# Silu of the normalised rows kept in its PSUM bank instead of an SBUF tile

## The reference

```
hn = rms_norm(x, norm_g)
a, b, gate = split(hn @ w_in, 3)                  # w_in 1024 x 3072
u = a * sigmoid(b)
u = depthwise causal conv (31 taps) of u + conv_b
u = (u - mean) * rsqrt(var + 1e-5) * ln_g + ln_b   # over the channels
u = silu(u) * silu(gate)
y = x + u @ w_out                                  # w_out 1024 x 1024
```

## The kernel before

| bank held by | passes to |
|---|---|
| `norm` 0, h = 0 | unit 23, half 0 |
| `norm` 1, 2, 3, h = 0 | `norm` 4, 5, 6, h = 0 |
| `norm` 4, h = 0 | unit 23, half 1 |
| `norm` 5, 6, h = 0 | `norm` 0, 1, h = 1 |
| `norm` 7, h = 0 | output `q` = 4 |
| `norm` k, h = 1 | `norm` k + 2, h = 1 |

## Time and profile before

### The profile page before, as it was taken

One profiled execution on the slowest core, in us unless ns is written; L12 is line 12 of the kernel. 1 busy time (PEld: TensorE's weight loads), 2 busy tenths in 40 slices (PEclk: granted clock), 3 DMA queues, 4 the chain that ended last, 5 costly groups with the idle time before them and its releaser, 6 DMA issues.

```text
span 387.0 us, 4783 instructions
## 1 busy us (share of the span) xinstructions
PE 377.4 (98%) x1704; PEld 305.5 (79%) x1704; DVE 277.4 (72%) x432; ACT 197.0 (51%) x301; POOL 243.2 (63%) x179
## 2 busy tenths in 40 slices
PE   3999999999999999999999999999999999999997
PEld 2788888888888888888888888888887888888886
DVE  4848899999998988999999999476248574011011
ACT  6869765576467517764685666444574650000000
POOL 0325999999999985999999999943423620000000
DMA  7993013111011111011111011110303558110111
GB/s 276 399 403 137 3 56 108 54 57 38 16 56 55 55 56 54 5 52 54 57 55 44 13 53 54 57 54 0 110 0 108 181 199 301 56 54 36 48 54 54
DMA packets 12263, 34.07 MB, mean 88 GB/s; under 512 B 1360, under 2 KB 1872, under 8 KB 12240
## 3 DMA queue, kind: packets, MB, share of 16 engines
q1 hardware_dynamic: 11952, 33.56, 24.2%
q10 hardware_dynamic: 288, 0.21, 0.3%
HBM read 29.57 MB, written 4.19 MB: 87 GB/s over the span
## 4 chain that ended last, share of the span: by engine, by line
PE 96%; DVE 1%; DMA 1%; ACT 0%; issue 0%; ACTq 0%; DVEq 0%
PE mm L433 64%; PE acc L506 17%; PE mm L506 7%; PE mm L450 5%; PE mm L489 2%; PE mm L500 2%; DMA ident<-identity 1%; DVE x_lo L818 1%; PE acc L427 1%; DVE w_lo L826 0%; ACT x_hi L570 0%; DVE nat L1031 0%; ACTq L558 0%; DVEq L817 0%
## 5 line engine op out<-in xcount | busy, mean ns | idle before, releaser
L433 PE MATMUL mm<-x_lo,w_hi 128*128 128x512 f32 x352 | 139.6, 397 | 0.0
L433 PE MATMUL mm<-x_hi,w_hi 128*128 128x512 f32 x352 | 139.3, 396 | 0.0
L433 PE MATMUL mm<-x_hi,w_lo 128*128 128x512 f32 x352 | 139.2, 396 | 0.0
L902 DVE SCALAR_TENSOR_TENSOR acc<-u,chan,acc 128x512 f32<-128x512 f32 x154 | 108.4, 749 | 0.1
L433 PEld LDWEIGHTS mm<-x_hi,w_hi 128*128 128x128 f32 x352 | 66.1, 188 | 16.1
L433 PEld LDWEIGHTS mm<-x_lo,w_hi 128*128 128x128 f32 x352 | 66.1, 188 | 15.6
L433 PEld LDWEIGHTS mm<-x_hi,w_lo 128*128 128x128 f32 x352 | 66.1, 188 | 15.5
L1102 POOL TENSOR_TENSOR pconv<-pconv,prod 128x512 f32<-128x512 f32 x60 | 77.3, 1313 | 0.4 <-ACT prod L658 0.4
L902 DVE SCALAR_TENSOR_TENSOR acc<-u,w_sum,acc 128x512 f32<-128x512 f32 x90 | 67.4, 749 | 0.2
L1065 POOL TENSOR_TENSOR w_lo<-raw,w_hi 128x1024 fp32r<-128x1024 f32 x21 | 51.0, 2427 | 20.5 <-ACT w_hi L608 20.4
L1102 POOL TENSOR_TENSOR pool_before<-pool_before,prod 128x512 f32<-128x512 f32 x41 | 53.5, 1304 | 1.6
(11 more groups left out here) (86 smaller groups left out, 449.9 us busy)
## 6 DMA issues: line engine op xcount, KB each, us to landing
raw<-w_in SPq DMA_DIRECT2D x22, 512.0 KB, 3.3
nat<-x_t SPq DMA_DIRECT2D x16, 256.0 KB, 6.1
sgate<-x SPq DMA_DIRECT2D x8, 512.0 KB, 10.7
raw<-w_out SPq DMA_DIRECT2D x8, 512.0 KB, 3.3
nat<-x SPq DMA_DIRECT2D x8, 512.0 KB, 6.0
y<-nat SPq DMA_DIRECT2D x15, 256.0 KB, 2.0
raw<-w_in SPq DMA_DIRECT2D x4, 256.0 KB, 4.7
y<-nat SPq DMA_DIRECT2D x2, 128.0 KB, 1.8
```

Of the source, the lines that this page charges most:

```text
L433: ins = nc.tensor.matmul(bank(("unit", m, h)), w[:, m % 3, k, :], xx[:, k, half(h)], start=(k == 0 and i == 0), stop=(k == KC - 1 and i == 2))
L902: ins = nc.vector.scalar_tensor_tensor(dst, chain_in(j, chain, k), tap(j, chain, k), chain_bank(j, chain), ALU.mult, ALU.add)
```

## The change

Silu is written over its own input, in the PSUM bank. The gate's product reads it from there. The wait for a free slot of `sig` is gone. The bank of a `norm` job is now released by the gate's product on DVE (`v_ready`, same count) and no longer by the Silu on ACT (`actv_ready`). No instruction is added, removed or moved on any engine; only operands and waits differ. The `sig` tile stays, since the first product's sigmoid uses it.

```diff
@@ release(job)
-            return actv_ready, KC * h + n + 1
+            return v_ready, KC * h + n + 1
@@ act_norm(k, h), ScalarE
                 act.wait_ge(nt_ready, n + 1)
-                if n >= 2:
-                    act.wait_ge(v_ready, n - 1)
-                nc.scalar.activation(sig[:, n % 2, :], bank(("norm", k, h)), ACT.Silu, scale=ln_g[:, k:k + 1],
+                nc.scalar.activation(bank(("norm", k, h)), bank(("norm", k, h)), ACT.Silu, scale=ln_g[:, k:k + 1],
                                      bias=ln_b[:, k:k + 1]).then_inc(actv_ready, 1)
@@ gate(k, h), VectorE
                 dve.wait_ge(actv_ready, n + 1)
                 dve.wait_ge(g_read, NH * k + h + 1)
-                nc.vector.tensor_tensor(sgate[:, k, part], sig[:, n % 2, :], sgate[:, k, part],
+                nc.vector.tensor_tensor(sgate[:, k, part], bank(("norm", k, h)), sgate[:, k, part],
                                         ALU.mult).then_inc(v_ready, 1)
```

## The result

The changed kernel took 390.14 us (median of 10 runs, 389.8 to 391.1), the kernel before 389.33 us (median of 10, 388.69 to 390.0). The ratio is 1.0022, its 95% interval 1.0012 to 1.0033: a little slower, +0.8 us, with an interval of +0.5 to +1.3 us. I had forecast +0.6 us and a time of 389.9 us in a range of 389.2 to 390.8. The difference is clear of zero, but the interval holds the bound of 0.2% (0.78 us) that the forecast had set between no change (0.49) and slower (0.45), so it does not settle on which side of it the change lies.

A forecast was written before the change was run, and what follows sets the result against it. PE, busy 98% of the span, was taken to bound the kernel. Two new waits less the absorbed gap, +0.58 + 0.57 - 0.54 = +0.61 us, gave 389.42 us profiled, 389.9 us median, range 389.2 to 390.8.

The forecast's parts named there:

- The sign, the place and the mechanism: Slower by 0.61 us, because PE newly waits for DVE's gates at both halves of unit 23.
- The absorbed gap: Before the output stage, PE's 0.54 us loss to late `x_lo` of k = 0 is given back.
- The rival that paid both waits in full: Gap before the output stage is really issue and stays: +1.15 us, 390.45 us; chance 0.22.
- S1: PE's new wait at unit 23 half 0 for the gate of k = 0: 0.58 us.
- S2: PE's new wait at unit 23 half 1 for the gate of k = 4: 0.57 us, on top of S1.
- the sum of +0.61: Whole kernel: two new waits at unit 23 less the gap before the output stage, +0.58 + 0.57 - 0.54 us.
- how far `x_lo` moves: Before the output stage, `x_lo` of k = 0 ends 0.27 us later, at 290.84 us.
- two passes: Rival: in-place Silu reads and writes its PSUM bank in turn, 1.27 us; +2.9 us, 392.2 us; chance 0.08.
- Not slower: Rival: unit 23's banks are free in time, only the earlier ACT remains; 388.5 us profiled, 389.0 median; chance 0.08.
- The other banks: Remaining `norm` banks at both h: released early enough, no further PE wait; nearest in h = 1 has some 1.7 us slack.
- the faster gates: Gates of h = 1 beside POOL fall from up to 2.49 to 0.69 us, hidden behind busy PE, worth nothing.

The follow-up runs named there:

- Experiment 1: Kernel before with only the bank release moved to the gate's product, Silu still to SBUF; median 390.10 us, ratio 1.0015.
- experiment 2: Changed kernel, but Silus of k = 0 and 4, h = 0, go to `sig` and release their banks themselves; median 389.22 us, ratio 0.9998.
- experiment 3: Changed kernel, but only the Silu of k = 4, h = 0, goes to `sig` and releases its bank; median 389.74 us, ratio 1.0013.
- experiment 4: Changed kernel, but only the Silu of k = 0, h = 0, goes to `sig` and releases its bank; median 389.63 us, ratio 1.0001.
- experiment 5: Kernel before with ScalarE's third and fourth `w_out` splits placed behind two and four `x_hi`; median 388.87 us, ratio 0.9993.
- experiment 6: Changed kernel with ScalarE's third and fourth `w_out` splits placed behind two and four `x_hi`; median 389.98 us, ratio 1.0021.
- Experiment 8: Changed kernel, but at unit 23 PE waits first for the bank, then for the weights' low part; 390.6 us in one run.

## Why the prediction was right, point by point

**The sign, the place and the mechanism held.** PE waits for the gates of k = 0 and k = 4, at the two places named, and for no other gate. Experiment 1 shows that the release alone makes the difference, experiment 2 that without the two waits it is gone.

**The absorbed gap held.** I had read the 0.31 us of "issue" as `x_lo` of k = 0 behind POOL, a loss of 0.54 us that one of the two waits would fill. Measured: -0.55 us, and experiments 3, 4 and 5 each show it from another side. The rival that paid both waits in full is out in the kernel as it is: that would be M = 15.48 + 1.28 = 16.76. Both waits in full, 1.28 us, are what experiments 5 and 6 differ by, once the gap has been removed.

**Mis-sized: S1 and S2.** They were 0.58 and 0.57 us, and are 0.64 each. The step that was too small is the time from DVE's end to the weight load. I took 0.06 us from the earlier trace rows; at unit 23 it is 0.12 (279.04 to 279.16). Experiment 8 shows that this depends on the order in which the two semaphores are waited for: the earlier trace rows is a wait behind one semaphore, unit 23 one behind two with the late one second. Why the order matters no run shows. The Silu's 0.04 us of shortening was 0.024 (776 to 752 ns), and the gates started 0.02 to 0.03 us earlier. Per wait that is some 0.07 us more than forecast, of which 0.06 to 0.07 show (0.64 against 0.58 and 0.57). With the gap's 0.55 in place of 0.54 it makes the 0.12 us by which M (+0.73) missed the sum of +0.61.

**Mis-sized, without effect: how far `x_lo` moves.** I had +0.27 us; from the first transpose to the end of `x_lo` of k = 0 it is 15.08 us before and 15.46 after, +0.38. Of the 0.11 us between them 0.06 are those of S1, 0.02 those of the Silus (0.29 us earlier and not 0.31), and 0.03 lie between the first `x_hi` and `x_lo` (0.65 us before, 0.68 after).

**The Silu.** 752 ns, neither the 736 I took nor the 1270 of two passes; that rival is out. The longer DVE access to PSUM, which the Trainium skill ("Perfetto Trace Analysis", Optimizing Scalar/DVE Operations) gives at 125 ns against 60, is not seen in the gate, 692 against 693 ns; for ScalarE it gives 51 against 93 ns, and of these 42 ns the Silu shows 24.

**Not slower.** This rival needed a gate's end before PE's weight load; the first gate ended at 279.04, and without the wait the load would have come at 276.88 + 1.63 = 278.51. It is out.

**The other banks and the faster gates.** No further wait of PE. The gates beside POOL fell from 2493 to 694 ns at most and DVE's busy time from 277.4 to 273.4 us, and that is worth nothing on the time (the stretch behind M is equal in all profiles).

**The time.** The median moved by 0.81 us, M by 0.73, the forecast was 0.61. With 0.2% at 0.78 us, the chances of no change and of slower stood nearly even for good reason; the 0.06 us in each wait, which I had read from a place with another kind of wait, would have brought the sum to the 0.73 that M shows, still just inside that bound.

## What to carry to other kernels

When a buffer's release moves from one engine to the next in the chain, list who takes each buffer over, and read for each how long before its need it was free: here PE waited for none of 14 gates, and the two whose bank had been free for under 0.2 us made the whole loss. Before adding up new waits of the bounding engine, look for a gap it has already: a wait fills it only if the cause of the gap doesn't move with the wait, as experiments 3 and 4 tell apart. And a short gap named "issue" is worth a look at what ended just before it; this one was a DVE instruction that took 1.8 us longer beside POOL than alone, and a later place for two ScalarE instructions takes it away.

## What the runs showed of the hardware that was not expected

**The order of two waits on PE.** With the late semaphore second of two, PE took up its work 0.12 us after DVE's end, with it first 0.04 us (experiment 8), 0.07 to 0.08 us less at the second matmul. Experiment 8 is one profile with two such places. Before the output stage, where the late semaphore is the second of three, the load comes 0.07 us after DVE's end.

**The opening differs from run to run.** The 1.39 us by which the changed kernel's profile starts late come from the first 14 us. DMA lets PE start at 7.03 instead of 6.47 us. Then the matmuls come every 0.43 us for longer; the step to one every 0.233 us is made at 13.5 us, against 10.4 us in the kernel before. The timeline of PE in the changed kernel:

```profile
12.67 0.63 PE L450 MATMUL mm<-x_hi,w_hi 128*128 128x512 f32 x1
13.10 0.55 PE L450 MATMUL mm<-x_lo,w_hi 128*128 128x512 f32 x1
13.48 0.40 PE L450 MATMUL mm<-x_hi,w_lo 128*128 128x512 f32 x1
13.72 0.40 PE L450 MATMUL mm<-x_hi,w_hi 128*128 128x512 f32 x1
```

The granted clock is printed as 1.00 in these stretches too, so the row of the clock does not show it; the matmuls' own durations do, 0.63 against 0.40 us. What sets the moment of the step no run here shows. Over the ten profiles the first transpose behind unit 22 half 1 lies between 275.49 and 276.88 us; none of the edits touches what runs ahead of it. What a change of under 1 us does can therefore be read from a stretch of one profile, as M, better than from its span.
